# Attention tiles turned by products with a diagonal, or scaled on ScalarE and turned by identity transposes

## The chip, the core and the metric

The kernel runs on one core of a Trainium2 chip. The core has TensorE (matrix products, called PE in the profile), VectorE (DVE), ScalarE (ACT), GpSimd (POOL) and SyncE (SP), each with its own queue of instructions, which wait for one another by semaphores. SBUF is the working memory, PSUM the eight banks into which TensorE writes. The metric is the time of one execution on the device in microseconds; a run's time is the median of several.

## The reference

Two blocks follow each other on 512 tokens of width 1024, in fp32. The first is a state-space mixer with a gated MLP. The second has two layers over a latent sequence of 512 tokens and a context of 256, and in it stands the attention that the change touches:

```python
s_win = einsum("bhqd,bhiqjd->bhqij", q_r, k_win) * scale + bias   # neighbourhood window
s_ctx = einsum("bhqd,bhcd->bhqc", q_r, k_ctx) * scale             # all context keys
p = jax.nn.softmax(concatenate([s_win, s_ctx]), axis=-1)
out = p_win @ v_win + p_ctx @ v_ctx                               # 8 heads of 64
```

`context_attention` is the same without the window, over the 256 context keys. Around it each layer has a convolution branch (31 taps per channel over a gated input, a layer norm), gates, output projections and a gated feed-forward part. All of it is computed in fp32.

## The kernel before

Weights come as a stream of units, each 128x1024 numbers, through a ring of four slots. A unit is split by ScalarE (`split_hi`, L251) and GpSimd (`split_lo`, L259) in a high and a low part, and TensorE makes three products of each 128x128 block (high by high, high by low, low by high). In the context pass of layer 0 the units are used whole, by plain fp32 products.

The mixing stage of a layer runs as a *pass*: `c0` (context, 256 tokens), `l0` and `l1` (latent, 512 tokens) hold attention. On each engine one function writes the pass down in full, `mix_pe`, `mix_act`, `mix_dve` and `mix_pool`, and the order of the code is the order of the queue.

The attention goes in *rounds* n. A round takes one pair of heads and one tile of 128 queries: 16 rounds in a latent pass, 8 in the context pass. For round n:

- `scores_pe`: products of queries and keys to banks 4 and 5 of PSUM, one bank per head, 512 columns (256 in the context pass).
- `top_dve`: VectorE adds the bias (latent) and takes the negative maxima.
- `exps_act`: ScalarE writes the exponentials to the SBUF tile `pex` and their sums to `sm`. It waits for the maxima and for the turn of the round before, since `pex` is a single tile.
- `scale_dve` (L2165): VectorE takes the reciprocals of the sums (L2168) and multiplies the identity with them (L2171), which gives two diagonal matrices `dg`.
- `turn_pe` (L1944): TensorE multiplies each 128x128 block of `pex`, as the stationary operand, with the diagonal of its head (L1951). The result in banks 6 and 7 is the block transposed and its columns scaled. 8 products in a latent round, 4 in a context round.
- `copied_act` (L2049): ScalarE copies both banks to `pT`, a single tile too, so it waits for the values of the round before.
- `values_pe` (L1970): the products with the values.

TensorE's queue in round n reads: scores(n), turn(n-1), values(n-2), then *filler* units of the weight stream (one in a latent round, two in the context pass), with the product or transposes that put q, k or v of the next heads in place (`pe_post`, L1914 transposes v with the identity). ScalarE's queue reads: eviction of the last filler of the round before with the split of the unit four ahead, copy of turn(n-1), exponentials of n, and the output of a pair of heads when it is complete. VectorE's reads: top(n), `post_dve` for q, k or v (rounds 0 to 9 of a latent pass), `scale_dve` of n, and then taps of the convolution (`conv_taps`, L2186), one tap of two tiles in rounds 0 to 9 of a latent pass and two taps in the others. GpSimd makes the taps of the two other tiles and the low parts of the weights. After the rounds TensorE runs six more units, VectorE the taps that are left and a sum (L2229, L2232), and the product for the mean (L2255) waits for both.

From round 8 of a latent pass on the fillers are gates, whose eviction is a sigmoid: ScalarE then loads a table before each gate and one before each pair of exponentials.

## Time and profile before

| | |
|---|---|
| time, median of 3 runs | 3050.27 us (3049.93 to 3056.47) |
| span of the profiled execution | 3030.3 us |
| TensorE busy | 2855.5 us, 94% |
| VectorE busy | 1568.4 us, 52% |
| ScalarE busy | 1068.2 us, 35% |
| GpSimd busy | 1266.1 us, 42% |
| chain that ended last | TensorE 76%, VectorE 10% and its queue 4%, ScalarE 3% |

The profiled execution shows its span, from the first to the last instruction; the timed runs also hold what lies around it, and their median is 20.0 us above the span. "PEld" is TensorE's weight load, which overlaps its products. "Idle before" names what ended the idle time of an engine. The chain of waits is followed back from the last instruction, at each step to what released it. The three attention stages lie near 1040 to 1135 us (`c0`), 1297 to 1480 us (`l0`) and 2308 to 2490 us (`l1`).

### The profile page before, as it was taken

What the parts mean: (1) busy time and instruction counts of PE and PEld (TensorE: products, weight loads), DVE (VectorE), ACT (ScalarE), POOL (GpSimd) and SP (SyncE); (2) the same over time, 40 slices, a digit from 0 to 9 for tenths busy, and PEclk for the clock granted to TensorE, in tenths of its full rate; (3) what the DMA queues carried; (4) which work ended last, traced back from release to release, by engine and by line L of the source; (5) the groups of instructions that cost most, each with busy time, mean ns of one, the idle gap of its engine ahead of it and who ended that gap; (6) DMA issues with size and microseconds to landing.
All of it is one profiled execution on the core that took longest, in us unless ns stands there. A gap on an engine that the chain in (4) does not pass through costs nothing.

```text
span 3030.3 us, 41702 instructions
## 1 busy us (share of the span) xinstructions
PE 2855.5 (94%) x15864; PEld 2327.7 (77%) x15864; DVE 1568.4 (52%) x2050; ACT 1068.2 (35%) x1579; POOL 1266.1 (42%) x696
## 2 busy tenths in 40 slices
PE   6999987999999998999989999999999998899997
PEld 6974745878888887777767888888787777688886
DVE  6875684451224463387765423423347876652525
ACT  4435233332333232335433322313343453342433
POOL 3452102443544370587623322222348773344443
PEclk9999998999999999999999999999999999999998
DMA  5327595322332333422221211221233212223332
GB/s 177 94 89 251 164 299 185 101 96 86 111 91 85 115 112 125 132 77 77 68 65 59 80 63 62 63 63 62 77 91 97 74 60 70 83 90 93 94 97 70
DMA packets 115578, 306.91 MB, mean 101 GB/s; under 512 B 36128, under 2 KB 44448, under 8 KB 114784
## 3 DMA queue, kind: packets, MB, share of 16 engines
q1 hardware_dynamic: 86000, 284.22, 29.7%
q10 hardware_dynamic: 28864, 18.76, 2.2%
q8 instruction: 102, 1.67, 0.2%
q0 software_dynamic: 560, 1.84, 0.2%
q14 instruction: 52, 0.43, 0.0%
HBM read 294.95 MB, written 7.45 MB: 100 GB/s over the span
## 4 chain that ended last, share of the span: by engine, by line
PE 76%; DVE 10%; DVEq 4%; ACT 3%; DMA 2%; issue 2%; POOL 1%; ACTq 1%; SPq 0%; POOLq 0%
PE ps L298 36%; PE ps L328 17%; PE ps L319 6%; PE ps L1893 3%; DVE co L2186 2%; PE ps L2299 2%; DVEq L2187 2%; PE ps L1951 2%; PE ps L1897 1%; DMA mt<-ka 1%; PE ps L1898 1%; PE ps L1901 1%; POOL wlo L259 1%; PE ps L715 1%; DVE mv L2378 1%
## 5 line engine op out<-in xcount | busy, mean ns | idle before, releaser
L259 POOL TENSOR_TENSOR wlo<-wraw,whi 128x1024 fp32r<-128x1024 f32 x373 | 923.3, 2485 | 1446.0 <-ACT whi L251 1444.5
L251 ACT ACTIVATE whi<-wraw 128x1024 fp32r<-128x1024 f32 x373 | 391.9, 1054 | 485.5 <-PE ps L328 157.8
L298 PE MATMUL ps<-xhi,whi 128*128 128x512 f32 (+1 forms) x1328 | 469.8, 370 | 1.7 <-issue 1.7
L298 PE MATMUL ps<-xlo,whi 128*128 128x512 f32 (+1 forms) x1328 | 470.6, 371 | 0.0
L298 PE MATMUL ps<-xhi,wlo 128*128 128x512 f32 (+1 forms) x1328 | 334.0, 371 | 0.0
L298 PEld LDWEIGHTS ps<-xhi,whi 128*128 128x128 f32 x1328 | 240.5, 188 | 48.1 <-issue 2.7
L298 PEld LDWEIGHTS ps<-xlo,whi 128*128 128x128 f32 x1328 | 240.5, 188 | 44.5
L298 PEld LDWEIGHTS ps<-xhi,wlo 128*128 128x128 f32 x1328 | 232.3, 188 | 44.7
L2186 DVE SCALAR_TENSOR_TENSOR co<-ub,vec,co 128x512 f32<-128x512 f32 (+1 forms) x216 | 226.9, 1090 | 6.1 <-issue 1.3
L2285 POOL TENSOR_TENSOR co<-co,ct 128x512 f32<-128x512 f32 (+1 forms) x144 | 164.8, 1144 | 20.5
L1076 DVE SCALAR_TENSOR_TENSOR res<-ps,mod,res 128x512 f32 (+1 forms) x64 | 47.7, 749 | 222.0 <-PE ps L319 132.2
L298 PE MATMUL ps<-hhi,whi 128*128 128x512 f32 x408 | 159.2, 390 | 1.8 <-DVE gt L2373 1.8
L298 PE MATMUL ps<-hlo,whi 128*128 128x512 f32 x408 | 158.8, 389 | 0.0
L2528 DVE SCALAR_TENSOR_TENSOR f<-ps,vec,f 128x511 f32<-128x511 f32 x88 | 50.2, 613 | 196.1 <-ACT f L2491 196.1
L1897 PE MATMUL ps<-xhi,whi 128*128 128x512 f32 x352 | 145.3, 413 | 4.2 <-DVE ub L2198 2.6
L2283 POOL TENSOR_TENSOR ct<-ub,vec 128x512 f32<-128x512 f32 (+1 forms) x144 | 133.8, 929 | 22.5 <-issue 12.3
L1898 PE MATMUL ps<-xlo,whi 128*128 128x512 f32 x352 | 139.5, 396 | 0.0
L328 PE MATMUL ps<-xhi,whi 128*128 128x512 f32 (+1 forms) x320 | 95.3, 388 | 11.8 <-ACT xhi L466 5.7
L1074 DVE TENSOR_TENSOR res<-res,ps 128x512 f32<-128x512 f32 x48 | 33.0, 688 | 132.1 <-PE ps L298 70.2
L298 PE MATMUL ps<-hhi,wlo 128*128 128x512 f32 x408 | 100.9, 389 | 0.0
L319 PE MATMUL ps<-xchi,whi 128*128 128x256 f32 x352 | 100.7, 286 | 0.0
L319 PE MATMUL ps<-xclo,whi 128*128 128x256 f32 x352 | 100.2, 285 | 0.0
(395 smaller groups left out, 5695.8 us busy)
## 6 DMA issues: line engine op xcount, KB each, us to landing
wraw<-stream SPq DMA_DIRECT2D x425, 512.0 KB, 3.5
wada<-w_ada SPq DMA_DIRECT2D x56, 512.0 KB, 7.6
wraw<-w_ada SPq DMA_DIRECT2D x40, 512.0 KB, 3.9
biasb<-attn_bias ACTq DMA_DIRECT2D x32, 256.0 KB, 3.8
xin<-x0T SPq DMA_DIRECT2D x4, 528.0 KB, 6.3
s_u<-uk ACTq DMA_DIRECT2D x8, 264.0 KB, 3.8
res<-x0T ACTq DMA_DIRECT2D x1, 2048.0 KB, 9.0
s_y<-yk ACTq DMA_DIRECT2D x64, 32.0 KB, 4.9
```

What stands on the lines that cost most here:

```text
L251: act.activation(whi[:, s], wraw[:, s], ACT.Copy).then_inc(hi_done[s], 1)
L259: pool.tensor_tensor(wlo[:, s], wraw[:, s], whi[:, s].bitcast(F32), ALU.subtract).then_inc(lo_done[s], 1)
L298: last = pe.matmul(ps[:, bank, 0:b - a], w[:, s, kt], x[:, kt, c0 + a:c0 + b], start=start, stop=stop)
L319: return pe.matmul(ps[:, R + s, 0:CTX], w[:, s, kt], part[:, kt], start=start, stop=stop)
L328: last = pe.matmul(ps[:, bank, 0:b - a], w[:, s, kt], x[:, kt, c0 + a:c0 + b], start=start, stop=stop)
L1893: last = pe.matmul(o, wraw[:, s, kt], x1[:, kt, 0:p.T], start=kt == 0, stop=kt == NT - 1)
L1897: pe.matmul(o, whi[:, s, kt], xhi[:, kt, 0:p.T], start=kt == 0, stop=False)
L1898: pe.matmul(o, whi[:, s, kt], xlo[:, kt, 0:p.T], start=False, stop=False)
L1951: last = pe.matmul(ps[:, 6 + h, b * P:(b + 1) * P], pex[:, h, b * P:(b + 1) * P], dg[h], start=True, stop=True)
L2186: dve.scalar_tensor_tensor(o, ub[:, m, k:k + p.T], colr(f"dw{p.l}", 1, k * 4 + m), o, ALU.mult, ALU.add)
L2283: pool.tensor_tensor(ct[:, 0:T], ub[:, m, k:k + T], colr(f"dw{l}", 1, k * 4 + m).to_broadcast([P, T]), ALU.mult)
L2285: ins = pool.tensor_tensor(o, o, ct[:, 0:T], ALU.add)
```

## The change

ScalarE gets a step `scale_act`: after the reciprocals it multiplies each head's exponentials in `pex`, in place, by the reciprocal of its row. VectorE keeps the reciprocal alone. TensorE's turn becomes a transpose with the identity. The two diagonal matrices go, and there is a new semaphore for the reciprocals.

```diff
-    dg0 = at("dg0", [P, P], O_C + 4 * CONST["tri"])
-    dg1 = at("dg1", [P, P], O_C + 4 * CONST["keep"] + 2048)
-    dg = (dg0[:, :], dg1[:, :])
...
@@ turn_pe
-                last = pe.matmul(ps[:, 6 + h, b * P:(b + 1) * P], pex[:, h, b * P:(b + 1) * P], dg[h], start=True, stop=True)
+                last = pe.transpose(ps[:, 6 + h, b * P:(b + 1) * P], pex[:, h, b * P:(b + 1) * P], ident)
...
+    def scale_act(act, p, n):
+        act.wait_ge(p.a_rec.sem, p.a_rec.past("reciprocal", n))
+        for h in range(2):
+            c = 2 * (n % 2) + h
+            ins = act.activation(pex[:, h, 0:p.W], pex[:, h, 0:p.W], ACT.Copy, scale=sm[:, 2, c:c + 1])
+        ins.then_inc(p.a_sc.sem, 1)
...
@@ mix_act, in round n
             for g in now[:-1]:
                 evac_act(act, p, g)
+            if n < p.N:
+                scale_act(act, p, n)
             late = now[-1:]
...
-    def scale_dve(dve, p, n):
+    def rec_dve(dve, p, n):
         c = 2 * (n % 2)
         dve.wait_ge(p.a_exp.sem, p.a_exp.past("exp", n))
-        dve.reciprocal(sm[:, 2, c:c + 2], sm[:, 1, c:c + 2])
-        dve.drain()
-        for h in range(2):
-            ins = dve.tensor_scalar(dg[h], ident, sm[:, 2, c + h:c + h + 1], None, ALU.mult)
-        ins.then_inc(p.a_sc.sem, 1)
+        dve.reciprocal(sm[:, 2, c:c + 2], sm[:, 1, c:c + 2]).then_inc(p.a_rec.sem, 1)
```

On ScalarE, round 13 of a latent pass (`pex` exponentials, `hhi` the output of a pair of heads, `gt` a gate, `whi` the high part of a unit, `pT` the turned tile). Before:

```order
L251 ACTIVATE whi<-wraw 128x1024
L2049 ACTIVATE pT<-ps 128x1024
L2059 ACT_TABLE_LOAD
L2059 ACTIVATE pex,sm<-ps,sm 128x512 x2
L2065 ACTIVATE hhi<-ps 128x64x8
L2031 ACT_TABLE_LOAD
L2031 ACTIVATE gt<-ps 128x512
L251 ACTIVATE whi<-wraw 128x1024
```

And after:

```order
L251 ACTIVATE whi<-wraw 128x1024
L2046 ACTIVATE pT<-ps 128x1024
L2056 ACT_TABLE_LOAD
L2056 ACTIVATE pex,sm<-ps,sm 128x512 x2
L2069 ACTIVATE hhi<-ps 128x64x8
L2063 ACTIVATE pex<-pex,sm 128x512 x2
L2028 ACT_TABLE_LOAD
L2028 ACTIVATE gt<-ps 128x512
L251 ACTIVATE whi<-wraw 128x1024
```

The two activations of line 2063 are new; they stand behind the exponentials and the output, and ahead of the gate and the split. No table load is added.

On VectorE, the same round (`sm` maxima, sums and reciprocals, `dg` the diagonals, `hlo` the low part of the output, `co` the taps). Before:

```order
L2163 TENSOR_REDUCE sm<-ps 128x2
L2168 RECIPROCAL sm<-sm 128x2
L2171 TENSOR_SCALAR dg_143<-cst,sm 128x128
L2171 TENSOR_SCALAR dg_144<-cst,sm 128x128
L2179 TENSOR_TENSOR hlo<-ps,hhi 128x64x8
L2186 SCALAR_TENSOR_TENSOR co<-ub,vec,co 128x512 x4
```

And after:

```order
L2166 TENSOR_TENSOR ps<-ps,biasb 128x2x256
L2169 TENSOR_REDUCE sm<-ps 128x2
L2174 RECIPROCAL sm<-sm 128x2
L2181 TENSOR_TENSOR hlo<-ps,hhi 128x64x8
L2188 SCALAR_TENSOR_TENSOR co<-ub,vec,co 128x512 x4
```

The two diagonal products between the reciprocal and the next work are gone.

On TensorE, the same round: scores (`kT`, `kctx`), turn and values. Before:

```order
L1939 MATMUL ps<-kT_140,qT_139 128x256 x2
L1941 MATMUL ps<-kctx,qT_139 128x256 x2
L1951 MATMUL ps<-dg_143,pex 128x128 x4
L1951 MATMUL ps<-dg_144,pex 128x128 x4
L1970 MATMUL ps<-pT,vT_138 64x128 x4
L1970 MATMUL ps<-pT,vctx 64x128 x4
```

And after:

```order
L1936 MATMUL ps<-kT_140,qT_139 128x256 x2
L1938 MATMUL ps<-kctx,qT_139 128x256 x2
L1948 MATMUL ps<-cst,pex 128x128 x8
L1967 MATMUL ps<-pT,vT_138 64x128 x4
L1967 MATMUL ps<-pT,vctx 64x128 x4
```

The eight products with diagonals are eight transposes with the identity (`cst`) in the same place of the queue.

## Rows read from the trace of the kernel before

**Rows 1.** Busy time by stretch: context rounds, latent rounds 3 to 9, 10 to 15

```profile
core 0: us, PE busy (x) PEld busy (x) DVE busy (x) ACT busy (x) POOL busy (x), PEclk, DMA share, GB/s
1040.00:1135.00 95.00, 94.37 (x509) 77.92 (x508) 57.78 (x93) 32.04 (x73) 77.44 (x116) 1.00 0.39 119
1330.00:1405.00 75.00, 75.00 (x485) 59.07 (x485) 62.49 (x95) 33.38 (x54) 51.78 (x35) 1.00 0.24 75
1405.00:1472.00 67.00, 63.79 (x412) 50.92 (x408) 44.66 (x54) 41.48 (x56) 49.42 (x34) 1.00 0.20 63
```

**Rows 2.** Chain of waits, a context round and latent round 9: start, us, what

```profile
1066.94 1.09 PE ps L1951 x8
...
1068.61 7.10 PE ps L1893 x32
...
1391.45 0.44 PE ps L1914 x4
1391.89 0.63 PE ps L1939 x4
1392.52 0.43 PE ps L1941 x4
1392.95 1.98 PE ps L1951 x16
1394.94 1.02 PE ps L1970 x16
```

**Rows 3.** Products with diagonals and identity transposes: count, ns min/median/max

```profile
L1951 PE MATMUL ps<-dg,pex x576: 272/275/377, 1058.0 to 2475.9; 128*128 128x128 f32 x192
...
L1825 PE MATMUL ps<-cst,gv x8: 271/272/273, 2278.3 to 2279.1; 128*128 128x128 f32 x8
```

**Rows 4.** Nearest operations on ScalarE and the diagonals on VectorE: the same columns

```profile
L920 ACT ACTIVATE st<-st,dca x48: 332/334/339, 219.8 to 269.6; 128x64 f32<-128x64 f32 x48
...
L2059 ACT ACTIVATE pex<-ps,sm x80: 463/680/692, 1051.2 to 2472.5; 128x512 f32<-128x512 f32 x64, 128x256 f32<-128x256 f32 x16
...
L2059 ACT ACT_TABLE_LOAD  x20: 1283/1283/1283, 1049.9 to 2468.2; - x20
...
L2171 DVE TENSOR_SCALAR dg<-cst,sm x80: 272/286/2437, 1052.5 to 2473.8; 128x128 f32<-128x128 f32 x80
```

**Rows 5.** TensorE in order of time, latent passes: instructions that waited, idle in brackets

```profile
1326.10 0.63 PE L1914 MATMUL ps<-cst,vraw 128*128 128x128 f32 x4 [0.65 <-DVE kT L2150]
...
1329.58 2.05 PE L1951 MATMUL ps<-dg,pex 128*128 128x128 f32 x16 [1.79 <-DVE dg L2171]
...
1422.04 0.70 PE L1939 MATMUL ps<-kT,qT 64*128 64x256 f32 x4 [0.72 <-ACT pex L2059]
...
1464.11 2.05 PE L1951 MATMUL ps<-dg,pex 128*128 128x128 f32 x16 [1.24 <-DVE dg L2171]
...
2337.89 0.63 PE L1914 MATMUL ps<-cst,vraw 128*128 128x128 f32 x4 [0.44 <-DVE kT L2150]
```

**Rows 6.** VectorE in order of time, latent round 14

```profile
1448.91 0.70 DVE L2160 TENSOR_TENSOR ps<-ps,biasb 128x512 f32<-128x512 f32 x1
1449.68 1.23 DVE L2163 TENSOR_REDUCE sm<-ps 128x2 f32<-128x1024 f32 x1
1452.42 0.17 DVE L2168 RECIPROCAL sm<-sm 128x2 f32<-128x2 f32 x1 [1.51 <-ACT pex L2059]
1452.67 1.30 DVE L2171 TENSOR_SCALAR dg<-cst,sm 128x128 f32<-128x128 f32 x2
1453.89 5.79 DVE L2186 SCALAR_TENSOR_TENSOR co<-ub,vec,co 128x512 f32<-128x512 f32 x4
```

**Rows 7.** End of the stage: VectorE's last taps, TensorE's product for the mean

```profile
1476.55 33.12 DVE L2186 SCALAR_TENSOR_TENSOR co<-ub,vec,co 128x512 f32<-128x512 f32 x26
...
1514.07 1.13 PE L2255 MATMUL ps<-lmu,cst 128*128 128x512 f32 x2
```

**Rows 8.** Busy time by stretch, eight transposes and a wait of TensorE

```profile
2278.30:2279.30 1.00, 1.00 (x9) 0.79 (x7) 0.10 (x1) 0.80 (x2) 0.00 (x0) 1.00 0.86 324
...
2305.00:2308.10 3.10, 0.39 (x2) 0.02 (x1) 2.96 (x4) 1.54 (x2) 2.94 (x3) 1.00 0.00 0
2308.10:2311.20 3.10, 3.09 (x13) 1.94 (x13) 0.00 (x0) 0.00 (x0) 2.81 (x3) 0.51 0.50 174
```

More of the change, by code:

```diff
@@ L1782, in __init__ @@
             self.c_g = s("conv_taps", "conv", passes=self.taps - 1)
-            self.a_s, self.a_max, self.a_exp, self.a_sc, self.a_turn, self.a_pt, self.a_pv = (
-                s(f"attn_{k}", k, passes=self.N) for k in ("scores", "max", "exp", "scaled", "turned", "copied", "values"))
+            self.a_s, self.a_max, self.a_exp, self.a_rec, self.a_sc, self.a_turn, self.a_pt, self.a_pv = (
+                s(f"attn_{k}", k, passes=self.N) for k in ("scores", "max", "exp", "reciprocal", "scaled", "turned", "copied", "values"))
             self.o_a, self.o_v = s("aout_hi", "hi", passes=4), s("aout_lo", "lo", passes=4 * two)
@@ L2218, in mix_dve @@
                     post_dve(dve, p, post_at[n])
-                scale_dve(dve, p, n)
+                rec_dve(dve, p, n)
             if out_due(p, n) is not None and not p.one:
```

## The prediction

> **What bounds the kernel now.** I read five views in this order: the busy times by stretch, the chain of waits over the three attention stages, the instructions of the lines touched, the order of time on each engine in single rounds, and the rows where TensorE waited. A *round* is one pass n of the attention loop: scores(n), turn(n-1), values(n-2), then one filler unit (two in the context pass). The context pass has 8 rounds, the latent passes 16 each.
>
> The busy times by stretch say that TensorE is the bound there: 94.37 of 95 us in the context rounds, 75.00 of 75 in latent rounds 3 to 9, 63.79 of 67 in rounds 10 to 15 [rows 1]. So what leaves TensorE's queue in a round leaves the time, until another engine is late. The waits of TensorE in the first latent pass [rows 5] say who that will be: 1.79 us for the diagonals in round 3, then in the last rounds 0.72 for the exponentials and 1.24 for the diagonals, some 3 us in all. VectorE's own loop (maxima, reciprocal, diagonals, four taps of the convolution) is already as long as TensorE's there. After the last values both tails are fixed and equal: VectorE has 26 tap instructions, 33.12 us, TensorE seven units, and the product for the mean follows them at 1514.07 without a wait, 4.4 us after the taps' end, the time that VectorE's sum of the tiles takes [rows 7]. Hence the whole gain of a latent pass is how much earlier its last values run.
>
> **The change part by part.**
>
> *TensorE.* A turn of a latent round is 8 products of 128x128. Each leaves two records (576 records for 288 products), and in the chain the turn holds 1.98 us [rows 2, 3], 0.25 us a product. In a context round four products hold 1.09 us [rows 2]. The transpose of the same type and shape, data as weights and the identity moving, is in the kernel already: one record each (8 records for the 8 of line 1825) [rows 3], and 4 in 0.44 us of the chain [rows 2], so 0.11 us each. The new turn is 0.88 us (8 x 0.11) and 0.44 us. Saved: 1.10 us x 32 = 35.2, and 0.65 us x 8 = 5.2; 40.4 us of queue.
>
> The Trainium skill (TensorE: Matmul & The Clock Gate, Terms) gives the transpose mode as 4 times as fast for fp32. By that estimate a latent turn would shrink to 0.5 us. The rows at 0.11 us against 0.25 us show 2.25 times for this shape, and they stand for the very instruction; the sum by the page would be some 9 us better, and I don't use it.
>
> *ScalarE.* Added: two activations per round, 512 columns (256 in the context), from SBUF to SBUF with a scale per partition. The nearest rows are the same form at 64 columns, 334 ns, and the exponential of 512 columns with a bias per partition, 680 ns [rows 4]. Bounds for one: 0.60 us (an activation without the accumulator's read may be cheaper) and 0.80. I take 0.70, and as back-to-back ones overlap, 1.33 us the pair. No table load comes with it: the copy of the turned tile is the same function and stands among the exponentials without one. ScalarE's round of 10 us then carries: table load 1.28, exponentials with reads 1.47, pair 1.33, table load 1.28, gate 0.5, weight split 1.05, copy 1.03 = 7.9 us, against a TensorE round of 8.7. It fits, so the term is 0 while the pair ends before TensorE asks for the turn. Queued behind the pair, which now waits for the reciprocal, are the filler's eviction and the split of weights four units ahead; the latter feeds GpSimd, which was busy 49.42 of 67 us [rows 1] and has the room.
>
> When does the pair land? In a round that VectorE does not delay, values(n-2) end 2.95 us after the scores start (1.06 + 0.88 + 1.02) [rows 2], then copy 1.15, exponentials 1.5, reciprocal and its hand-over 0.3, pair 1.4: 7.3 us. With the table load of 1.28 us ahead of the exponentials [rows 4] it is 8.6. The turn is asked for at 8.7 + 1.06 = 9.8 us (9.6 + 1.06 with the q and k products in rounds 3 to 9). Slack 1.2 to 3.4 us. In a context round the first of two fillers (7.10 us together [rows 2]) ends 5.2 us after the scores start, its eviction and hand-over at 5.8, the pair of 0.9 at 6.7, or 8 with a gate's table load; the turn is asked for at 9.4. Hidden.
>
> *VectorE.* Removed: the drain and the two diagonal products, 286 ns at the median and up to 2437 [rows 4]. From the reciprocal's end to the first tap the row-by-row gap is 1.22 us in round 14 [rows 6], and 0.39 us where nothing interferes (two of 286, overlapped). I take 0.9 a round; the ends are 0.4, if the next tap inherits the delay, and 1.2.
>
> *The sum for a latent pass.* Up to the start of round 10, TensorE is the bound: nine turns, 9.9 us. In the first latent pass the wait of 1.79 us goes too: in rounds 0 and 1 VectorE and TensorE both come about 2.2 us earlier, and the pair of round 2 then ends as the scores of round 3 do. The wait of 0.65 us for kT [rows 5] stays, as its chain is VectorE's. In the second latent pass that place shows only 0.44 us for kT [rows 5] and no wait for diagonals. So round 10 starts 11.7 and 9.9 us earlier. From there VectorE's loop decides the last turn: five rounds x 0.9 = 4.5 us more, less 0.8, because that turn waits for a pair and hand-overs of 1.6 us where it waited for diagonals of 0.8. Then the last turn itself, 1.1. That is 11.7 + 4.5 - 0.8 + 1.1 = 16.5 and 9.9 + 4.5 - 0.8 + 1.1 = 14.7. TensorE's account alone would give 17.6 each; the difference reappears as waits before turns and scores of the last six rounds.
>
> Context pass: 5.2, in full, since TensorE is full there [rows 1] and every other engine has the slack above.
>
> All: 16.5 + 14.7 + 5.2 = 36.4 us. The profiled execution's span is 3030.3, so 2993.9 after; the median of the runs shown is 20.0 us above that span, and 3050.3 - 36.4 = **3014 us**.
>
> **The rivals.**
>
> *VectorE takes it back in the late rounds.* The diagonals' long times come from what GpSimd does beside them: a product of 0.29 us lasts up to 2.4, about the length of a GpSimd weight split. If the tap that follows inherits that, and the same taps of GpSimd crowd into a shorter stretch, the late rounds give nothing: 4.5 us less per pass, 36.4 - 9.0 = 27.4, time 3023. For it: the four tap instructions of round 14 take 5.79 us [rows 6], 1.45 each, against 1.27 in the tail [rows 7]. Against: GpSimd idles a quarter of that stretch.
>
> *All waits vanish.* The late waits, 3.1 us in each latent pass [rows 5], and the 1.8 go with TensorE's full 40.4: 40.4 + 1.8 + 6.2 = 48.4, time 3002. It needs VectorE's loop under TensorE's 8.7 us, against bias and maxima 2.0, wait for the exponentials 1.5, reciprocal 0.25 [rows 6] and four taps at the tail's 1.27, 5.1: 8.85. It is possible in some rounds, hardly in all.
>
> *The transposes cost what the products do.* Then only VectorE's relief is left, about 2 us; time 3048. Against it are 48 transposes of two lines here at one record each. That is the rival in which the change doesn't do what it says.
>
> *Slower: ScalarE becomes the bound of the late rounds.* Place: its 7.9 us a round with two table loads. VectorE's operations in SBUF stretch beside GpSimd, 0.29 to 2.44 us [rows 4]; if the new activations, which no longer read PSUM, did the same, ScalarE's round would grow with them. At 3.0 us each its round is 12.6 us against TensorE's 8.7, 12 such rounds lose 47 us, and 47 - 36.4 = 11 us slower: 3061. It decides from 2.6 us each on. Against it: no ACTIVATE of the listed forms leaves its narrow band, 463 to 692 ns over two shapes, 332 to 339 ns within SBUF [rows 4].
>
> *Slower by the clock.* In a stretch of 3.1 us in which TensorE worked for 0.39, nothing fell yet; in the next 3.1 us the granted clock was 0.51, its lower level of 1.2 GHz, and half of the stretch was lost, 1.5 us [rows 8]. If each turn of transposes brought that about, 32 x (1.5 + 0.9 for the turn itself - 1.1) = 42 us would be lost, less some 5 of the context: 3087. But eight transposes in a row were granted 1.00 [rows 8]. The Trainium skill (TensorE: Matmul & The Clock Gate, Part 4) says that transposes do not count as busy for that gate. By that rule a turn could bring the clock down; the trace gives it no support, and a turn of 0.88 us stands between products in rounds that are otherwise full.
>
> **How the numbers follow.** Forecast 0.60; VectorE takes it back 0.22; all waits vanish 0.10; no gain from transposes 0.03; ScalarE late 0.03; clock 0.02. The likeliest gives 3014. Its unknowns are the diagonals' 0.4 to 1.2 a round (5 us each way), the pair, and a wait or two. The range holds the first three cases: 3001 to 3026. What can be told from no change is about 0.2%, 6 us: faster 0.92, within 0.04, slower 0.04.
>
> **What the profile after would show.** Line 1948 should stand with 288 records and hold 0.88 us per latent turn. Line 2063, two a round, near 0.7 us each. Rounds 3 to 9 at 9.6 us (9.2 where v is turned), with TensorE without waits. In rounds 12 to 15 waits of TensorE for the exponentials or the pair, 1 to 2 us each, 6 in a pass. The last taps should still be 26 and about 33 us. I would be wrong if TensorE waits for line 2063 in rounds 3 to 9, if the taps of the late rounds grow by more than a microsecond a round, if the mean after the units waits for VectorE by more than 1 us, or if the granted clock falls below 1.00 within the rounds.

## The result, and the profile after

| | before | after |
|---|---|---|
| median, 6 runs each, taken together | 3050.1 us (3032.25 to 3056.47) | 3021.17 us (3017.59 to 3026.05) |
| ratio, 95% interval | | 0.9926 (0.9907 to 0.9944), 22.5 us less |
| span of the profiled execution, its run | 3030.3 us | 3015.8 us, a run of 3017.59 |

The kernel is faster, by 22.5 us and not by the 36.4 forecast; 0.9926 of 3050.3 is 3028, outside the range of 3001 to 3026. The two medians lie further apart, 28.9 us, and the lower one, 3021, would lie inside that range. I go by the ratio, because the stages below add up to 22.7 us and the kernel after, timed once more, gave 0.9923. Single executions of one kernel differ by some 25 us here (before: 3032 to 3056 us), and the context pass of these profiles starts anywhere from 1050 to 1067 us, so below I compare stages within a pass and leave the spans alone.

The busy times by stretch, in order the context rounds, latent rounds 3 to 9, rounds 10 to 15, and the end after the last turn. The columns are those of [rows 1].

```profile
1060.00:1150.00 90.00, 89.37 (x471) 73.08 (x471) 44.95 (x70) 36.45 (x85) 66.17 (x99) 1.00 0.40 123
1330.00:1395.00 65.00, 64.59 (x398) 49.08 (x397) 56.12 (x75) 39.25 (x66) 51.40 (x33) 1.00 0.26 80
1395.00:1454.00 59.00, 54.41 (x340) 41.38 (x339) 43.38 (x44) 49.20 (x71) 46.79 (x32) 1.00 0.23 70
1454.00:1505.00 51.00, 47.90 (x232) 38.24 (x231) 45.05 (x34) 16.91 (x21) 34.12 (x19) 1.00 0.27 83
```

Rounds 3 to 9 take 66.9 us where they took 75.0 [rows 1], and TensorE is still full there. In rounds 10 to 15 it now idles 4.6 of 59 us (before 3.2 of 67), and GpSimd, with the same work in less time, is busy 79% of that stretch against 74%.

The groups for the lines touched (count, ns min/median/max), and beneath line 1948 what ended the idle time before it:

```profile
L1948 PE MATMUL ps<-cst,pex x288: 271/273/478, 1064.0 to 2460.7; 128*128 128x128 f32 x144
...
  ACT pex L2063: 11.8, 19
...
L2063 ACT ACTIVATE pex<-pex,sm x80: 495/708/740, 1060.3 to 2458.8; 128x512 f32<-128x512 f32 x64, 128x256 f32<-128x256 f32 x16
...
L2188 DVE SCALAR_TENSOR_TENSOR co<-ub,vec,co x216: 464/942/2952, 1047.5 to 2505.1; 128x512 f32<-128x512 f32 x78, 128x256 f32<-128x256 f32 x30
```

Line 1948 has the 288 records forecast and line 2063 costs 0.71 us, as forecast. The 11.8 us count the queue of weight loads too; TensorE's products waited for line 2063 for 2.4 us in the first latent pass and 1.2 in the second. A turn is read in TensorE's order of time as the distance from its start to the start of the values behind it. A context turn, and the latent turn of round 13:

```profile
1072.35 0.66 PE L1948 MATMUL ps<-cst,pex 128*128 128x128 f32 x4
1072.93 0.66 PE L1967 MATMUL ps<-pT,vctx 128*64 128x128 f32 x8
...
1436.45 1.09 PE L1948 MATMUL ps<-cst,pex 128*128 128x128 f32 x8 [0.91 <-ACT pex L2063]
1437.47 0.66 PE L1967 MATMUL ps<-pT,vT 128*64 128x128 f32 x8
```

That is 0.58 us (before 1.08, from 1066.87 to 1067.95) and 1.02 us (1.98 [rows 2]). TensorE's waits in the first latent pass up to the mean, in sum, times, longest:

```profile
PE ps L1911 <- DVE kT L2156: 4.6, 3, 2.7
PE ps L2257 <- DVE lmu L2234: 2.4, 1, 2.4
PE ps L1948 <- ACT pex L2063: 2.4, 4, 0.9
PE ps L1936 <- ACT pex L2056: 2.1, 2, 1.5
PE ps L1913 <- DVE vT L2138: 1.3, 1, 1.3
```

Against before, the 3.5 us for diagonals in three places are gone. New are 2.4 us for the pair of line 2063, all of it in the late rounds, and 2.4 at the mean, where none was. The wait for kT of 2.7 stands ahead of the first scores in both kernels; that ahead of the scores of round 3 grew from 0.65 [rows 5] to 1.50.

The 1.3 us for v look new as well, but they don't come from the change. In the profile before, TensorE ran the weight products of round 0 in this pass at the lower clock, behind its wait of 2.72 us for kT, and in the profile after it did not. First before, then after:

```profile
1298.10:1301.30 3.20, 3.20 (x10) 2.52 (x9) 2.93 (x5) 0.47 (x1) 2.92 (x4) 0.51 0.33 131
```

```profile
1300.40:1303.90 3.50, 3.50 (x17) 2.89 (x16) 3.25 (x6) 0.81 (x1) 3.22 (x4) 1.00 0.32 120
```

Round 0 takes 9.19 us before and 9.21 after: what the clock takes in one profile, the wait for v takes in the other. In e0_after, the kernel after timed again, the clock is 0.54 in this place, there is no wait for v, and the round takes 9.24.

### Where it came from, stage by stage

In us. "Scores n" is the start of the scores of round n over the context keys. A pass starts at scores 0; "last turn" is the start of its last turn, "mean" that of the product for the mean. Saved is the difference of the two profiles.

| stretch | forecast saved, l0 / l1 | before, l0 / l1 | after, l0 / l1 | saved, l0 / l1 |
|---|---|---|---|---|
| scores 0 to scores 3 | 2.2 / 2.2 | 29.7 / 28.9 | 29.4 / 30.4 | 0.3 / -1.5 |
| to scores 10 | 9.5 / 7.7 | 75.0 / 73.1 | 66.9 / 67.7 | 8.1 / 5.4 |
| to the last turn | 3.7 / 3.7 | 61.9 / 62.0 | 57.7 / 58.7 | 4.2 / 3.3 |
| to the mean | 1.1 / 1.1 | 50.0 / 50.6 | 51.3 / 50.4 | -1.3 / 0.2 |
| pass | 16.5 / 14.7 | 216.6 / 214.6 | 205.3 / 207.2 | 11.3 / 7.4 |
| context pass | 5.2 | 104.4 | 100.4 | 4.0 |

The sum is 22.7 us, close to the measured 22.5 (0.9926). So the gain is made in these stages, and what is missing from the forecast is missing here. TensorE itself now needs 0.96 us less a latent turn and 0.50 less a context turn: 32 x 0.96 + 8 x 0.50 = 34.7. So 12 us that TensorE saved did not shorten the kernel.

### The profile page after: what moved, and what is told of

It is laid out like the page before. It is cut to its first block, busy times and chain, and to the rows that moved or that the text cites. A ratio compares the mean times of both kernels' runs of the same rounds, so it can differ in the third digit from the quotient of the medians.

```text
span 3015.8 us, 41087 instructions
## 1 busy us (share of the span) xinstructions
PE 2833.2 (94%) x15576; PEld 2299.8 (76%) x15576; DVE 1555.5 (52%) x1970; ACT 1114.2 (37%) x1659; POOL 1268.9 (42%) x696
## 3 DMA queue, kind: packets, MB, share of 16 engines
q1 hardware_dynamic: 86000, 284.22, 29.7%
## 4 chain that ended last, share of the span: by engine, by line
PE 75%; DVE 9%; DVEq 4%; ACT 4%; DMA 2%; issue 2%; ACTq 1%; POOL 1%; SPq 0%; POOLq 0%
PE ps L298 36%; PE ps L328 18%; PE ps L319 6%; PE ps L1890 3%; DVEq L2189 2%; PE ps L2301 2%; DVE co L2188 2%; PE ps L1894 1%; PE ps L1895 1%; PE ps L1898 1%; POOL wlo L259 1%; DMA mt<-ka 1%; DMA wraw<-stream 1%; DVE mv L2380 1%; PE ps L715 1%
## 5 line engine op out<-in xcount | busy, mean ns | idle before, releaser
L2188 DVE SCALAR_TENSOR_TENSOR co<-ub,vec,co 128x512 f32<-128x512 f32 (+1 forms) x216 | 247.0, 1183 | 5.4 <-issue 0.4
L2490 ACT ACTIVATE f<-ps,vec 128x512 f32<-128x512 f32 x44 | 34.3, 780 | 186.5 <-PE ps L319 178.5
L319 PE MATMUL ps<-xchi,whi 128*128 128x256 f32 x352 | 100.7, 286 | 0.0
```

Of the source, the lines that this page charges most:

```text
L319: return pe.matmul(ps[:, R + s, 0:CTX], w[:, s, kt], part[:, kt], start=start, stop=stop)
L2188: dve.scalar_tensor_tensor(o, ub[:, m, k:k + p.T], colr(f"dw{p.l}", 1, k * 4 + m), o, ALU.mult, ALU.add)
```

## The experiments

Each kernel was compared with the kernel before on the same chip. Of e5 and e6 there are only two runs each, of the others 6 to 12. The output of e3, e4, e5 and e6 is not the reference's, as each leaves work out. The passes (start to mean, from the profile of one execution):

| kernel | ratio, 95% interval | c0 | l0 | l1 |
|---|---|---|---|---|
| e0_after, the kernel after again | 0.9923 (0.9899 to 0.9948) | 100.4 | 206.1 | 207.2 |
| e1_ident_product | 0.9968 (0.9953 to 0.9983) | 104.4 | 211.2 | 209.7 |
| e3_no_pair | 0.9912 (0.9888 to 0.9937) | 100.4 | 207.0 | 206.5 |
| e4_transposes_alone | 0.9979 (0.9963 to 0.9995) | 100.4 | 212.5 | 214.7 |
| e5_before_short_taps | 0.9918 (0.9892 to 0.9944) | 104.4 | 208.3 | 208.3 |
| e6_after_short_taps | 0.9800 (0.9769 to 0.9830) | 100.4 | 193.2 | 193.2 |
| e7_gpsimd_24 | 0.9982 (0.9968 to 0.9996) | 100.4 | 215.2 | 216.3 |
| e9_late_taps | 0.9966 (0.9953 to 0.9979) | 100.4 | 212.8 | 210.9 |
| e10_taps_earlier | 0.9916 (0.9893 to 0.9938) | 100.4 | 208.7 | 205.8 |
| e11_two_taps_earlier | 0.9914 (0.9894 to 0.9935) | 100.4 | 204.0 | 203.0 |
| e2_diagonals_kept | 0.9960 (0.9947 to 0.9974) | 100.4 | 208.8 | 208.7 |
| e12_three_products | 0.9945 (0.9931 to 0.9960) | 100.4 | 207.0 | 209.3 |
| e13_taps_and_products | 0.9918 (0.9899 to 0.9938) | 100.4 | 207.2 | 207.6 |

How finely a single profile's pass can be read: between the two profiles of the kernel after, stretches differ by up to 1.9 us and passes by 0.8. Two later kernels, e11 and e13, have the same instructions up to round 12 of a pass and still reach scores 10 of the second latent pass after 95.4 and 100.7 us. So 2 us in one pass prove nothing by themselves, and 5 hardly do.

### The kernel after once more

> The changed kernel again, timed beside the others. Its earlier ratio to the kernel before is 0.9926, 22.5 us. Both theories: 20 to 26 us faster. Stage by stage the profiles gave 4.0 us in the context pass, 11.3 in the first and 7.3 in the second latent pass; the theory that VectorE is held by GpSimd expects TensorE to wait in rounds 1 to 3 for kT, qT or vT and after the units for the sum of the taps, the theory that ScalarE's pair comes late expects the larger waits at line 1948.

3020.85 us against 3042.78 (23 runs of before), ratio 0.9923. Its passes save 22 us. The result stands, and the place too. Between the two theories it does not decide: in the first latent pass TensorE waits 1.9 us for kT behind the first scores and 2.4 at the mean against 1.7 for line 2063, in the second 4.5 for line 2063. e3 below does.

### What the instruction is worth: the same turn as a product

```diff
-                last = pe.transpose(ps[:, 6 + h, ...], pex[:, h, ...], ident)
+                last = pe.matmul(ps[:, 6 + h, ...], pex[:, h, ...], ident, start=True, stop=True)
```

> The changed kernel, but the turn is an ordinary fp32 product with the identity: ScalarE's pair and VectorE's relief are in, TensorE's saving is out. Theory V (the relief is inherited by the next VectorE instruction that GpSimd holds up): within 3 us of the kernel before. Theory of the forecast (the relief is worth 0.9 us a round in the late rounds): 5 to 9 us faster. Theory P (the pair is late): 3 to 8 us slower than before.

3034.39 us, ratio 0.9968, 10 us faster than before (5 to 14 by the interval). The context pass goes back to exactly 104.4, and the turn back to two records a block and 1.98 us:

```profile
L1948 PE MATMUL ps<-cst,pex x576: 273/275/377, 1072.1 to 2479.7; 128*128 128x128 f32 x192
```

So moving the scale away from VectorE gives 10 us with the products kept (5.4 and 4.9 in the latent passes, 0 in the context pass), and the transposes give the other 12. Theory V, within 3 us of before, falls; the theory of the forecast, 5 to 9, lies within the interval. The prediction itself, in its rival without a gain from transposes, had put about 2 us on VectorE's relief alone. It overlooked that TensorE's own waits for diagonals and exponentials go with it: they are 3.5 + 1.4 and 1.7 + 1.4 us in the two latent passes before, and none is left in this run.

### Whether ScalarE's pair costs anything

```diff
-            if n < p.N:
-                scale_act(act, p, n)
...
-        dve.reciprocal(...).then_inc(p.a_rec.sem, 1)
+        dve.reciprocal(...).then_inc(p.a_sc.sem, 1)
```

> The changed kernel without ScalarE's pair; the exponentials are not scaled, so the output isn't the reference's; the turn waits for the reciprocal alone. Theory P: the waits for the pair go, 5 to 9 us faster than the changed kernel. Theory V: VectorE still decides, 0 to 3 us faster than the changed kernel, since it then waits for the exponentials instead.

This kernel leaves the scaling out. 3019.93 us, ratio 0.9912, against 0.9923 of e0_after; the intervals overlap, and the passes are 207.0 and 206.5 against 206.1 and 207.2. Forty pairs of 1.3 us are hidden, as forecast. The waits for line 2063 in the late rounds are thus not the pair's doing: without it the passes are as long, so what is late comes before the pair, at VectorE or at the exponentials.

### Transposes without the new division of work

```diff
-                last = pe.matmul(ps[:, 6 + h, ...], pex[:, h, ...], dg[h], start=True, stop=True)
+                last = pe.transpose(ps[:, 6 + h, ...], pex[:, h, ...], ident)
```

> The kernel before with its turn alone changed to transposes; the diagonals are made but not used, so the output is not scaled. TensorE saves 0.96 us a latent turn and 0.53 a context turn, 35 us of its queue. Theory V: the same as the changed kernel within 3 us, 20 to 25 us faster than before, because the diagonals cost nothing of their own. Theory of the forecast: 5 to 9 us slower than the changed kernel. Theory P: 3 to 8 us faster than the changed kernel.

The kernel before with this line alone; the diagonals are still made and waited for, and the output isn't scaled. 3037.15 us, ratio 0.9979. TensorE has the full 34.7 us less to do, and 8.0 us arrive: 4.0 in the context pass, 4.1 and -0.1 in the latent ones. Theory V, within 3 us of the kernel after, falls; the kernel is some 15 us slower than that one, more than the 5 to 9 of the forecast's theory. TensorE now waits 5.4 and 7.9 us for the exponentials in the latent passes, where the kernel after waits 2.1 and 2.7. Another part of the answer is in two rows of the stretches of its round 3, the turn and the values behind it:

```profile
1342.43:1344.26 1.83, 1.83 (x9) 1.50 (x9) 1.83 (x2) 0.00 (x0) 1.66 (x2) 0.54 0.45 63
1344.26:1346.30 2.04, 2.04 (x18) 1.77 (x18) 1.82 (x3) 0.02 (x1) 1.90 (x2) 0.58 0.52 209
```

Behind a wait of 1.73 us for the diagonals the granted clock is 0.54, the lower level of 1.2 GHz, and the turn takes 1.83 us instead of 1.02. Five of the 32 latent turns of this profile take 1.48 to 1.90 us, three in the first latent pass and two in the second. I come back to it below.

### The diagonals kept as dead work

```diff
+        dve.drain()
+        for h in range(2):
+            dve.tensor_scalar(dg[h], ident, sm[:, 2, c + h:c + h + 1], None, ALU.mult)
```

> The kernel after, with VectorE still making the two diagonal matrices behind each reciprocal, where nothing reads them. It shows what VectorE's relief is worth beside the transposes. Theory (VectorE held up by GpSimd decides where TensorE's saving arrives): the transposes keep their 1.02 us a turn, but a latent pass gives back 3 to 6 us in the rounds and at the end, so 8 to 13 us slower than the kernel after, near the kernel that had the transposes alone (0.998 of before, 8 us). Rival (what was forecast: only the late rounds are VectorE's, 0.9 us a round): 4.5 us a latent pass, 9 in all, with rounds 0 to 9 unchanged to within 0.5 us. Second rival (GpSimd's share is fixed and the next tap takes over the delay): under 3 us in all.

3028.87 us, ratio 0.9960, against 0.9923: by the ratios 11 us slower, with intervals that just touch; by the passes 2.7 and 1.5 us slower than e0_after. The ratio fits the theory's 8 to 13, the passes fit the forecast's smaller sum better, and the size is not settled by this. The place is: scores 10 comes after 96.1 and 95.2 us, as without the diagonals (96.4 and 95.4), and the loss is all behind it. Two more VectorE instructions in rounds 0 to 9 cost nothing, as the rival had it; in the late rounds they cost 3.6 and 2.4 us, of which 0.6 and 0.8 come back in the tail. Its distance from e4 is about what it is worth that nothing *waits* for diagonals any more: 3.7 and 6.0 us by the passes, 6 us by the ratios. Which of the two is worth more, the work removed or the wait removed, is open: the passes say the wait, the ratios (11 us against 6) say the work.

### GpSimd out of the way

```diff
-                pool.tensor_tensor(ct[:, 0:T], ub[:, m, k:k + T], ...)
...
-                ins = pool.tensor_tensor(o, o, ct[:, 0:T], ALU.add)
+                w = 8 if p.lat else T
+                o = co[:, m, 0:w]
+                pool.tensor_tensor(ct[:, 0:w], ub[:, m, k:k + w], ...)
...
+                ins = pool.tensor_tensor(o, o, ct[:, 0:w], ALU.add)
```

> The kernel before, but GpSimd's taps of the convolution in the latent passes work on 8 columns in place of 512, so its output isn't the reference's. It is the base for the next run; what counts is each latent pass from its first scores to the product for the mean (216.6 and 214.6 us in the kernel before). Theory G (GpSimd's taps hold VectorE up): shorter than before, by 5 to 15 us a pass, TensorE then full. Theory W (VectorE has too much work of its own): within 2 us of before.

> The changed kernel with GpSimd's taps of the latent passes on 8 columns, output not the reference's. Theory G: with GpSimd out of the way TensorE's whole saving arrives, 0.96 x 16 = 15.4 us a latent pass against the run e5, both passes alike within 1 us, and no wait of TensorE after the units. Theory W: the same 7 to 11 us a pass that the change gives with the taps in full.

Both leave out most of GpSimd's convolution in the latent passes: its taps work on 8 columns instead of 512. Before with that edit: 3019.88 us, ratio 0.9918. After with it: 2983.89, ratio 0.9800. The latent passes go from 208.3 to 193.2, twice the same 15.1 us, which is TensorE's own saving of 16 x 0.96 = 15.4. Two stretches of e6's first latent pass, about rounds 3 to 9 and 10 to 15:

```profile
1311.00:1380.00 69.00, 69.00 (x423) 52.59 (x422) 43.36 (x84) 41.15 (x69) 27.23 (x39) 1.00 0.28 88
1380.00:1435.00 55.00, 55.00 (x345) 42.28 (x344) 30.89 (x45) 50.42 (x72) 19.16 (x30) 1.00 0.24 73
```

TensorE does not idle in them at all, and VectorE, with the same instructions, is busy 30.89 of 55 us. With the taps at full length, the 24 VectorE taps of rounds 10 to 15 took 27.8 us before and 32.8 after in the first latent pass; here they take 17.3. This settles where the gain went: 15.1 us a pass arrive without GpSimd's taps, 11.3 and 7.4 with them. No wait of TensorE's products in the latent passes of the kernel after is for GpSimd itself, so the missing 4 and 8 us are VectorE made late beside GpSimd, and what follows from it. It also shows what the GpSimd taps cost the kernel before by themselves: 8.3 and 6.3 us a pass.

How one engine holds the other is seen in the first latent pass, where VectorE no longer makes the diagonals of round 0 and yet is little ahead. GpSimd's and VectorE's order of time in round 1, after:

```profile
1311.79 2.38 POOL L259 TENSOR_TENSOR wlo<-wraw,whi 128x1024 fp32r<-128x1024 f32 x1
1312.72 2.00 DVE L2143 TENSOR_TENSOR raw<-raw,cst 128x512 f32<-128x512 f32 x1
...
1314.64 0.68 DVE L2144 TENSOR_TENSOR rt<-ps,cst 128x512 f32<-128x512 f32 x1
```

The same operation before:

```profile
1311.73 0.75 DVE L2137 TENSOR_TENSOR raw<-raw,cst 128x512 f32<-128x512 f32 x1
```

The product from two SBUF operands takes 0.75 us by itself and 2.00 when it comes upon GpSimd's split: the split ends at 1314.17, the product 0.55 us later, about the time it needs by itself. The next one, which reads PSUM and SBUF, keeps 0.68 beside a GpSimd tap, and the maxima before it, which read PSUM, keep their 1.23 while the same split starts beside them. In round 2, whose k TensorE waits for, it is the same again: VectorE starts 1.57 us behind the scores, where it had started 2.92 behind them, and L2143 takes 1.99 us in place of 0.73, so that k is ready hardly earlier (9.74 us behind the scores, before 9.85). The Trainium skill (GPSIMD Engine Reference, section 1, Specifications) says that GpSimd shares its SBUF interfaces with VectorE, with contention for VectorE's instructions in a 2-port perf mode or with two SBUF inputs. These rows agree. The price by the rows is the rest of the running GpSimd instruction.

### Fewer taps ahead of time, or more on GpSimd

```diff
-                some(1 if p.lat and n < 10 else 2)
+                some(0 if p.lat and n < 3 else 1 if p.lat and n < 10 else 2)
```

> The changed kernel without VectorE's tap in rounds 0 to 2 of a latent pass; its six instructions run in the tail instead. Theory V (VectorE decides rounds 0 to 3): scores of round 3 come 2 to 4 us earlier, and the tail, which VectorE ends too, takes 6 x 1.3 = 8 us more, so the whole is 4 to 6 us slower a pass than the changed kernel. Rival, that TensorE decides the first rounds: round 3 comes no earlier, the tail the same 8 us longer.

3033.47 us, ratio 0.9966. Six tap instructions, about 7 us of VectorE, leave rounds 0 to 2, and these rounds hardly get shorter: 29.4 us in the first latent pass, as before the edit, and 27.7 against 28.5 (e0_after) in the second. The taps come back at the end, where the stretch from the last turn to the mean grows from 51.2 and 51.9 (e0_after) to 57.6 and 56.9. So theory V's 2 to 4 us in front do not come, though the passes are longer than those of e0_after by 6.7 and 3.7 us, near the 4 to 6 it had said. GpSimd and VectorE in the first latent pass, in order of time, and the one wait of TensorE in its rounds 0 to 2:

```profile
1310.45 2.39 POOL L259 TENSOR_TENSOR wlo<-wraw,whi 128x1024 fp32r<-128x1024 f32 x1
...
1310.59 2.34 DVE L2138 COPY vT<-vT 64x128 f32<-64x128 f32 x1
...
1318.03 2.41 POOL L259 TENSOR_TENSOR wlo<-wraw,whi 128x1024 fp32r<-128x1024 f32 x1
...
1318.49 2.50 DVE L2143 TENSOR_TENSOR raw<-raw,cst 128x512 f32<-128x512 f32 x1
...
1326.54 2.40 POOL L259 TENSOR_TENSOR wlo<-wraw,whi 128x1024 fp32r<-128x1024 f32 x1
...
1327.10 2.38 DVE L2143 TENSOR_TENSOR raw<-raw,cst 128x512 f32<-128x512 f32 x1
...
1335.01 0.63 PE L1911 MATMUL ps<-cst,vraw 128*128 128x128 f32 x4 [2.08 <-DVE kT L2156]
```

Each time VectorE runs into a split of 2.4 us and comes out behind it (1312.93 behind 1312.84, 1320.99 behind 1320.44, 1329.48 behind 1328.94). The first two cost TensorE nothing: it waits for nothing in rounds 0 and 1 (the first at the lower clock in part, 0.54 for 3.6 us), and VectorE waits 2.05 and 2.17 us for its scores, so the rival, that TensorE decides there, holds for these two. The third stands in the preparation of the k that the scores of round 3 need, and TensorE waits 2.08 us for it. The 0.6 us won in round 1 are lost again in round 2.

```diff
-POOL_TAPS = 22
+POOL_TAPS = 24
```

> The changed kernel with two more taps of tiles 0 and 1 in the latent passes on GpSimd (23 instead of 21), so that VectorE's tail has 22 tap instructions in place of 26. Theory V (the tail of a latent pass ends with VectorE): 1.3 to 2.9 us a pass less after the last turn, where TensorE's units then end last, 2 to 5 us in all against the changed kernel. Rival: GpSimd's extra work holds the other taps up and nothing is gained.

3040.23 us, ratio 0.9982: of the gain, some 17 us are lost, so theory V falls and the rival is right, by more than it had said. VectorE's taps in the tail, and TensorE at the mean:

```profile
1490.99 14.18 DVE L2188 SCALAR_TENSOR_TENSOR co<-ub,vec,co 128x512 f32<-128x512 f32 x8 [10.05 <-POOL co L2287]
...
1514.15 2.07 PE L2257 MATMUL ps<-lmu,cst 128*128 128x512 f32 x2 [10.54 <-DVE lmu L2234]
```

VectorE waits 10.05 us for GpSimd to finish, and all of it stands again at the mean. With `POOL_TAPS` at 22 that wait does not exist; the two engines are balanced within a tap or two, so nothing is to be had by giving GpSimd more.

### Taps into VectorE's idle time

```diff
-                some(1 if p.lat and n < 10 else 2)
+                some(1 if p.lat and (n < 10 and n not in (4, 6, 8) or n in (12, 14)) else 2)
```

> The kernel after, with VectorE's taps of the latent passes shared out anew: rounds 4, 6 and 8 take two taps (four instructions) instead of one, rounds 12 and 14 one instead of two, and so one tap less is left for the end. The number of taps and all else stay. Theory (VectorE, held up by GpSimd, sets the last rounds and the tail; in rounds 3 to 9 it idles 9 of 67 us): TensorE's waits of the last rounds, 4.5 us in the first latent pass, and the 2.4 us before the mean fall by about half, rounds 3 to 9 grow by at most 1 us, so 2 to 4 us less a latent pass than the kernel after, about 6 us in all, ratio to before about 0.990. Rival (the idle time of VectorE in rounds 3 to 9 is not free, because its chain of reciprocal, q, k and v preparation is what TensorE waits for next): rounds 3 to 9 grow by 2 to 5 us and the total is the same as after or up to 6 us slower.

3018.36 us, ratio 0.9916. The second latent pass is at 205.8; the first at 208.7 is longer than before the edit. Its rounds 3 to 9 grew from 66.9 to 70.3, and the wait at the mean fell from 2.4 to 0.9 us. Of the rest, 2.0 us are in rounds 0 to 2 (31.4 against 29.4), which the edit does not touch; a turn there lost its clock. Between theory and rival: the late waits went down, and most was paid in front.

```diff
-                some(1 if p.lat and n < 10 else 2)
+                some(1 if p.lat and n < 10 and n not in (6, 8) else 2)
```

> The kernel after, with rounds 6 and 8 of the latent passes at two taps instead of one and so two taps (four instructions, some 5 us) less at the end; rounds 10 to 15 unchanged. Theory (the tail is VectorE's): the stretch from the last turn to the mean falls from 51.3 us to TensorE's own 48.9, so about 2.4 us less in the first latent pass and 1.6 in the second, no more, as the late rounds keep their waits. Rival (VectorE's idle time in rounds 3 to 9 is not free): those rounds grow by 1 to 3 us and nothing or less is left.

3015.06 us, ratio 0.9914. Passes of 204.0 and 203.0, 2 and 4 us less than e0_after; from the last turn to the mean 48.7 us in both, so TensorE's units alone decide there, as expected, and no wait at the mean is left. VectorE's tail in the first pass:

```profile
1483.02 12.18 DVE L2188 SCALAR_TENSOR_TENSOR co<-ub,vec,co 128x512 f32<-128x512 f32 x8 [1.25 <-POOL co L2287]
1495.62 11.73 DVE L2188 SCALAR_TENSOR_TENSOR co<-ub,vec,co 128x512 f32<-128x512 f32 x10 [0.42 <-issue]
```

It now waits a little for GpSimd, and the mean is not held up by that. By the profile this is the best of the kernels that do all the work; by the ratios it can't be told from the kernel after (0.9914 with 0.9894 to 0.9935, against 0.9923 with 0.9899 to 0.9948).

### The clock behind a wait

In e4 turns behind waits ran at half clock. The kernel after has such turns too: in e0_after's first latent pass (the turn in order of time, and its stretch):

```profile
1442.00 1.97 PE L1948 MATMUL ps<-cst,pex 128*128 128x128 f32 x8 [0.92 <-ACT pex L2063]
```

```profile
1442.00:1443.90 1.90, 1.90 (x8) 1.57 (x9) 1.82 (x3) 1.89 (x3) 0.00 (x0) 0.50 0.04 9
```

In before, no turn of either pass took more than 1.99 us, not even the one behind a wait of 1.79 us [rows 5]. That suggested that the fall takes transposes behind the wait. The rule of the Trainium skill weighed in the prediction (TensorE: Matmul & The Clock Gate, Part 4: transposes don't count as busy) would bring the same. Against it stands the stretch of before shown above, 0.51 in weight products behind a wait, with no turn in it. Two kernels put products back where the late waits are, e12 in round 2 too:

```diff
-                last = pe.transpose(...)
+                if p.lat and n in (2, 13, 14):      # e13: (13, 14), with the taps of e11
+                    last = pe.matmul(ps[:, 6 + h, ...], pex[:, h, ...], ident, start=True, stop=True)
+                else:
+                    last = pe.transpose(...)
```

> The kernel after, with the turns of rounds 2, 13 and 14 of the latent passes made as fp32 products with the identity (8 products, 1.98 us instead of 1.02) and all others left as transposes. In the profiles so far every turn of 1.3 to 1.9 us with values of 2.1 us behind it, where the granted clock stood near 0.55, was a turn by transposes that came behind a wait of TensorE of 1.5 to 5 us; products behind the same waits kept 1.00 (before: 1.79 us, clock 1.00; transposes alone: 1.73 us, clock 0.54). Theory C (a wait followed by transposes lets the clock fall, a wait followed by products does not): no turn of rounds 2, 13 and 14 falls to the lower clock, granted clock 1.00 in both latent passes, against one event a pass of about 1.9 us in the kernel after; the products cost 0.96 us each where TensorE does not wait and nothing where it waits for VectorE next, so a latent pass of 205 to 207 us as before the edit, within 1.5 us. Rival (the clock falls with the wait alone, whatever follows): the products of those rounds take about 3.9 us instead of 1.98 in the rounds with a wait, and a pass is 2 to 4 us longer.

> The kernel after, with the two edits that looked best or equal so far: rounds 6 and 8 of the latent passes at two taps of VectorE, so two taps less at the end, and the turns of rounds 13 and 14 as products with the identity. Theory C with the tail's: the stretch from the last turn to the mean stays at TensorE's 48.7 to 49 us, no turn of rounds 13 and 14 loses its clock (with transposes one did in each pass, 1.90 us instead of 1.02), and the pass comes to 202 to 204 us, the same as or 1 to 2 us less than with the taps alone (204.0 and 203.0); ratio to before 0.990 to 0.992. Rival (clock falls with the wait alone): 205 to 207 us a pass.

3027.0 us, ratio 0.9945, and 3018.88 us, ratio 0.9918. TensorE around the turn of round 13 in the first latent pass, e12 in order of time and as a stretch:

```profile
1435.31 0.70 PE L1936 MATMUL ps<-kT,qT 64*128 64x256 f32 x4 [1.30 <-ACT pex L2059]
...
1437.36 3.51 PE L1949 MATMUL ps<-cst,pex 128*128 128x128 f32 x16 [0.91 <-ACT pex L2066]
```

```profile
1437.40:1440.80 3.40, 3.40 (x17) 3.18 (x18) 3.18 (x5) 2.75 (x3) 0.56 (x1) 0.54 0.00 0
```

And e13:

```profile
1436.13 0.70 PE L1936 MATMUL ps<-kT,qT 64*128 64x256 f32 x4 [1.30 <-ACT pex L2059]
...
1438.17 2.05 PE L1949 MATMUL ps<-cst,pex 128*128 128x128 f32 x16 [0.91 <-ACT pex L2066]
```

```profile
1438.20:1440.20 2.00, 2.00 (x18) 1.88 (x18) 1.93 (x4) 1.99 (x3) 0.00 (x0) 1.00 0.03 8
```

My theory falls. The products of e12 lose the clock just as transposes do, 3.43 us instead of 1.98, so transposes aren't needed for it. And the rival falls in its plain form too: with the same two waits of 1.30 and 0.91 us and the same instructions, e13 keeps 1.00. A wait of TensorE in these rounds sometimes brings the clock down; what decides between the two I can't say from these traces. What it costs is clear: 0.9 us on a turn of transposes, 1.45 on one of products, and some 0.8 on the values behind (in e4 two groups of 1.12 and 1.00 us where they take 0.66 and 0.61). Putting products back gains nothing: e12 is at 0.9945 and e13 at 0.9918, and the intervals of both overlap those of the kernels with transposes. That this rule of the Trainium skill plays a part is neither shown nor excluded.

## Why the prediction was wrong

Point by point, by its own steps.

**A new turn costs 0.88 us, four of it 0.44: wrong in size.** It is 1.02 and 0.58. The 0.11 us for one more transpose holds, (1.02 - 0.58) / 4, but a run of them has 0.14 us besides. I had taken it from a run of four in the chain [rows 2], and the chain counts an instruction from the end of the one before it, 1391.45, to its own end. In order of time these four start at 1391.29, under the products before them, and the next instruction comes 0.53 us later:

```profile
1391.29 0.60 PE L1914 MATMUL ps<-cst,vraw 128*128 128x128 f32 x4
1391.82 0.70 PE L1939 MATMUL ps<-kT,qT 64*128 64x256 f32 x4
```

My own rows had the right size for eight as well, 1.00 us [rows 8]. The error is 32 x 0.14 + 8 x 0.15, 5.7 us of the 13.7 missing. The context pass, in which TensorE waits for no engine in either kernel, confirms the size: 4.0 us measured, 8 x 0.50.

**Rounds 0 to 2 come 2.2 us earlier: wrong.** The scores of round 3 came 0.3 us earlier in the first latent pass and not at all in the second (-1.5 us, and 0.4 in e0_after). I counted VectorE's relief there in full. It ran into GpSimd's next instruction instead, as the rival "VectorE takes it back" had it for the late rounds. I had also let the wait for kT stay at 0.65 us; it grew to 1.50, nearly the 0.96 that the turn of round 2 saved, and e9 shows that even 7 us less of VectorE's own work hardly shorten these rounds. Price: 1.8 to 3.7 us a pass, of the latter 1.9 with the clock.

**Rounds 3 to 9 are TensorE's: right.** 8.1 us against seven turns of 0.96 and the wait of 1.8 that went, 8.5; in the second pass 5.4 (6.2 in e0_after) against 6.7. TensorE stays full (64.59 of 65 us), and it does not wait for line 2063 there.

**Late rounds give 0.9 a round, less 0.8: right in sum.** 4.2 and 3.3 us against 3.7. The waits did appear, of 0.3 to 1.5 us (2.0 in the second pass), as VectorE's loop decides. e2 says that the diagonals were worth 3.6 and 2.4 us here by the passes. The rival has its part here too: the 24 taps of these rounds took 27.8 and 28.3 us before, 32.8 and 29.2 after and 29.0 and 31.1 in e0_after. That is 0.2 to 0.8 us a round, less than the microsecond that I had named as a sign against me.

**Both tails are fixed and equal, so the last turn's gain arrives: wrong.** The 26 taps that took 33.12 us [rows 7] take 37.5:

```profile
1452.33 7.64 DVE L2188 SCALAR_TENSOR_TENSOR co<-ub,vec,co 128x512 f32<-128x512 f32 x4
...
1465.31 25.46 DVE L2188 SCALAR_TENSOR_TENSOR co<-ub,vec,co 128x512 f32<-128x512 f32 x16
1491.20 11.57 DVE L2188 SCALAR_TENSOR_TENSOR co<-ub,vec,co 128x512 f32<-128x512 f32 x10 [0.43 <-issue]
```

VectorE's tail was as long as TensorE's already (in the second latent pass before, the mean waited 0.68 us for it), and the taps stretch with what GpSimd does beside them. The stretches of the 26 taps, first of before, then of after (GpSimd's is the fifth busy time):

```profile
1476.55:1509.67 33.12, 32.28 (x141) 26.02 (x140) 32.16 (x27) 8.94 (x12) 19.22 (x10) 1.00 0.30 92
```

```profile
1465.31:1502.77 37.46, 36.59 (x158) 29.23 (x156) 36.14 (x27) 9.28 (x12) 23.05 (x11) 1.00 0.28 85
```

GpSimd works 3.8 us more beside them, VectorE takes 4.3 us longer, and the mean waits 2.38 us at 1505.12 where it waited for nothing. This is the third sign that I had named against me, and it came. e11 removes it by two taps taken from the end.

**ScalarE's pair is hidden: right,** by e3, and its 0.71 us was within the bounds.

**VectorE's relief alone is worth 2 us (the third rival): wrong.** e1 measured 10 us, because TensorE's waits for diagonals and exponentials go with it.

**The clock: dismissed too quickly.** My fourth sign came as well. The granted clock falls to its lower level within rounds at single turns, none to two a pass in the kernels that scale on ScalarE and up to three in e4 (in the profile after 0.53 for 2.9 us behind the wait for kT in the second latent pass, its rounds 0 to 2 being 1.9 us longer than in e0_after, which kept it). But the kernel before does it too, in round 0 (0.51), so the sign told less than I thought. It is not the 32 turns of the rival. Each fall at a turn of these profiles stands at or behind a wait of TensorE, and a new wait can so cost up to about 2 us beyond itself.

**The time of 20.0 us around the span: wrong.** I set the span of one execution against the median of others. In every run here that has both, 1.7 to 1.9 us lie around the span, so the profiled execution of before was one of some 3032 us, an estimate. The rest was spread between runs. It did not touch the forecast difference.

In all, by the table: of the 13.7 us missing, rounds 0 to 2 hold 5.6 (4.4 forecast, -1.2 measured), rounds 3 to 9 3.7, the stretch after the last turn 3.3 (2.2 forecast, -1.1 measured), the context pass 1.2, and the late rounds none. The turn's size is in all of them, 5.7 us in sum; the other 8 are VectorE beside GpSimd and the clock behind the waits that come of it. e5 and e6 show for the whole pass that they go when GpSimd's taps go. What the waits cost by themselves and what by the clock is not separated.

## What to carry to other kernels

When TensorE gets faster in a kernel with a second engine near its limit, ask at what distance the other engines follow, and count the gain only up to the first place where one of them is waited for. An instruction taken off a VectorE that works beside GpSimd can give less than its own measured time, since the next one may run into the same GpSimd instruction. A step that TensorE waits for, moved to an engine without that conflict, took those waits with it (e1). Price a short run of instructions by the time from its start to the start of the next different one, not by its piece in the chain of waits or by a multiple of one.

## What the hardware showed

- Eight fp32 identity transposes of 128x128 take 1.02 us and four take 0.58; eight fp32 products of the same size take 1.98. A transpose leaves one record, a product two.
- A VectorE instruction of 0.75 us on SBUF operands took 2.00 when it came upon a GpSimd split of 2.38 us, ending 0.55 us behind it. The maxima, which read PSUM, kept their 1.23 us with the same split beside them, and the instruction that reads PSUM and SBUF kept 0.68 beside a GpSimd tap.
- ScalarE's activations within SBUF were not touched: 0.495 us at the least, 0.708 at the median and 0.740 at the most with GpSimd's taps in full, 0.495, 0.709 and 0.727 with them cut to 8 columns.
- The granted clock fell to about 0.54 at turns at or behind waits of 0.9 to 5 us in some executions and stayed at 1.00 behind the same waits in others, with products as with transposes. In the kernel before it was 0.51 in weight products behind a wait of 2.72 us.
- Two kernels with the same instructions up to round 12 can settle in different courses: 95.4 and 100.7 us to scores 10 of the second latent pass.
